# Per-head softmax over selected keys: maxima found two heads ahead, four tables each for keys and queries, a ring of three bias tiles

## What is computed

```python
def dsa_attention(q, k, v, qi, ki, wi, rel_bias, n_keep):
    def block(args):                       # 128 queries at a time
        ...
        _, idx = lax.top_k(score, n_keep)
        ksel = gather(k, idx); vsel = gather(v, idx)
        rel = qpos[None, :, None] - idx
        bias = jnp.moveaxis(rel_bias[t5_bucket_2(rel)], -1, 2)
        logits = jnp.einsum('bqhd,bqkhd->bqhk', qb, ksel) * (A_HEAD_DIM ** -0.5)
        logits = jnp.where((rel >= 0)[:, :, None, :], logits + bias, -jnp.inf)
        p = jax.nn.softmax(logits, axis=-1).astype(v.dtype)
        return jnp.einsum('bqhk,bqkhd->bqhd', p, vsel)
```

## Time and profile before

| | |
|---|---|
| median of 3 executions | 2489.11 us (2487.56 to 2490.77) |
| the profiled execution, first to last instruction | 2486.1 us |
| the stage's loop in it, first score to last mix | about 1133.8 to 1215.9 us, 82 us |
| busy over the whole span | PE 94%, PEld 87%, DVE 43%, ACT 40%, POOL 26% |
| mean granted TensorE clock | 0.968 |

### The profile page before, as it was taken

How to read it: one execution, slowest core, us unless ns; L and a number is a source line. 1 busy time by engine, 2 the same in 40 slices (tenths; PEclk the granted TensorE clock), 3 DMA queues, 4 the chain that set the end, 5 groups by cost and what they waited for, 6 DMA issues and landing times. The chain is left out here.

```text
span 2486.1 us, 40279 instructions
## 1 busy us (share of the span) xinstructions
PE 2329.6 (94%) x17224; PEld 2161.8 (87%) x17224; DVE 1076.9 (43%) x1571; ACT 987.5 (40%) x1440; POOL 647.8 (26%) x505
## 2 busy tenths in 40 slices
PE   7997898997899999898999999998999999999999
PEld 6995588985589997796799999998888879999998
DVE  2438624537532114596534434433334333543443
ACT  5237543246633325425524313324544433432332
POOL 1002222112222704436304302313221211320331
PEclk9999999998999999998999999999999989999999
DMA  5323022310022220122033233322111002323322
GB/s 179 117 90 93 1 69 81 97 54 5 1 90 69 69 78 18 52 77 78 27 98 89 75 101 93 88 88 85 35 35 38 32 33 70 99 74 109 94 73 81
DMA packets 235233, 175.94 MB, mean 71 GB/s; under 512 B 7732, under 2 KB 230060, under 8 KB 234544
## 3 DMA queue, kind: packets, MB, share of 16 engines
q1 hardware_dynamic: 235056, 173.37, 23.1%
HBM read 171.20 MB, written 10.09 MB: 73 GB/s over the span
## 5 line engine op out<-in xcount | busy, mean ns | idle before, releaser
L326 DVE TENSOR_TENSOR panel_lo<-panel_raw,panel_hi 128x2048 fp32r<-128x2048 f32 (+2 forms) x150 | 327.7, 2185 | 421.1 <-ACT panel_hi L318 421.1
L318 ACT ACTIVATE panel_hi<-panel_raw 128x2048 fp32r<-128x2048 f32 (+2 forms) x155 | 276.1, 1781 | 431.3 <-PE product L407 295.9
L407 PE MATMUL product<-scaled_hi,panel_hi 128*128 128x264 f32 (+2 forms) x1408 | 287.4, 285 | 8.3 <-DVE scaled_lo L3645 5.4
L420 PE MATMUL product_banks<-panel_hi,scaled_hi 128*128 128x256 f32 x1008 | 284.8, 282 | 4.0 <-DVE scaled_lo L3645 3.2
L407 PE MATMUL product<-scaled_lo,panel_hi 128*128 128x264 f32 (+2 forms) x1408 | 285.2, 284 | 0.0
L420 PE MATMUL product_banks<-panel_hi,scaled_lo 128*128 128x256 f32 x1008 | 284.7, 282 | 0.0
L420 PE MATMUL product_banks<-panel_lo,scaled_hi 128*128 128x256 f32 x1008 | 284.4, 282 | 0.0
L407 PE MATMUL product<-scaled_hi,panel_lo 128*128 128x264 f32 (+2 forms) x1408 | 284.2, 283 | 0.0
L407 PEld LDWEIGHTS product<-scaled_hi,panel_hi 128*128 128x128 f32 x1408 | 218.6, 190 | 9.1 <-issue 5.8
L407 PEld LDWEIGHTS product<-scaled_lo,panel_hi 128*128 128x128 f32 x1408 | 219.1, 189 | 0.0
L407 PEld LDWEIGHTS product<-scaled_hi,panel_lo 128*128 128x128 f32 x1408 | 218.8, 190 | 0.0
(11 more groups left out here) (478 smaller groups left out, 5309.7 us busy)
## 6 DMA issues: line engine op xcount, KB each, us to landing
panel_raw<-in_w_in_dram SPq DMA_DIRECT2D x26, 1024.0 KB, 5.3
panel_raw<-in_ffn_w_gate_dram SPq DMA_DIRECT2D x44, 512.0 KB, 4.0
panel_raw<-in_ffn_w_up_dram SPq DMA_DIRECT2D x44, 512.0 KB, 5.3
panel_raw<-in_ffn_w_down_dram SPq DMA_DIRECT2D x32, 704.0 KB, 4.5
panel_raw<-in_even_w_in_dram SPq DMA_DIRECT2D x21, 1024.0 KB, 5.1
panel_raw<-in_odd_w_in_dram SPq DMA_DIRECT2D x12, 1024.0 KB, 5.1
panel_raw<-in_w_out_dram SPq DMA_DIRECT2D x8, 1024.0 KB, 5.1
panel_raw<-in_even_w_out_dram SPq DMA_DIRECT2D x8, 768.0 KB, 4.7
```

The source lines that it names most:

```text
L318: act.activation(c.hi[g % 2][:, 0:used], c.raw[g % 2][:, 0:used], ACT.Copy).then_inc(c.hi_made.sem, 1)
L326: dve.tensor_tensor(c.lo[g % 2][:, 0:used], c.raw[g % 2][:, 0:used], c.hi[g % 2][:, 0:used].bitcast(F32), ALU.subtract).then_inc(c.lo_made ...
L407: done = pe.matmul(to, weight(w, k), a[:, k, u:v], start=(k == 0 and x == 0), stop=(k == chunks - 1 and x == 2))
L420: done = pe.matmul(out[:, 0, 0:v - u], a[:, k, at:at + P], w[:, k, u:v], start=(k == 0 and x == 0), stop=(k == chunks - 1 and x == 2))
```

## The change

Four edits.

1. **The maxima are scored two heads ahead.** In iteration i the PE scores head i+2, where it scored i+1. The loops start at i = -2. DVE's `largest` goes with the scores and `low_query`, `key_high` and `query_high` are called for head i+3. `keys` and `query` become rings of four (two more tables of their own in SBUF; the pads of eight tables are cleared in place of six).
2. **The turning moves.** `turn_max(i+1)` stands first in PE's iteration i, so behind `mix(i-2, 4)` and `mix_first(i-2)` of the iteration before it. It turns what was scored in the iteration before.
3. **The copy of the row moves with it.** `max_row(i+1)` stands first in ACT's iteration i, ahead of `take_first(i-2)` and `logarithm(i-2)`. `score_keys(i, 1)` waits for it as well (the count at `min(i+2, H)`), and `turn_max(h)` waits for `sum_added` at 2(h-1), since both use the spare columns of `z`.
4. **`row_bias` becomes a ring of three.** `add_mask` of tile n waits for `largest` of tile n-3, where it waited for n-2.

So in after i = -2 and -1 hold scores alone, i = 0 scores and `score_keys`, i = 1 to 5 all three, i = 6 and 7 `score_keys` and `mix`, i = 8 `mix` alone. POOL's order of work is as it was.

```diff
@@ -2115,15 +2115,16 @@
+    ROWS = 3
...
         slot = [t[:, PAD * n:PAD * (n + 1)] for t in (*c.hi, *c.lo) for n in range(3)]
-        slot += [c.sb(f"selected_slot{n}", [P, PAD], F32R, into=stage)[:] for n in range(2)]
-        keys, query, keys_low, query_low = slot[0:3], slot[3:6], slot[6:10], slot[10:14]
+        slot += [c.sb(f"selected_slot{n}", [P, PAD], F32R, into=stage)[:] for n in range(4)]
+        keys, query, keys_low, query_low = (slot[4 * n:4 * n + 4] for n in range(4))
...
         e = [c.sb(f"selected_e{j}", [P, Stick.WIDE], into=stage) for j in range(2)]
-        row_bias = [c.sb(f"selected_bias{j}", [P, TOK], into=stage) for j in range(2)]
+        row_bias = [c.sb(f"selected_bias{j}", [P, TOK], into=stage) for j in range(ROWS)]
@@ -2176,12 +2177,13 @@
...
                         v = min(u + 512, x)
-                        done = pe.matmul(scores[:, at + u:at + v], query[h % 3][:, b * P:(b + 1) * P], keys[h % 3][:, u:v], start=True, stop=True)
+                        done = pe.matmul(scores[:, at + u:at + v], query[h % 4][:, b * P:(b + 1) * P], keys[h % 4][:, u:v], start=True, stop=True)
                     done.then_inc(c.head_scored.sem, 1)

                 def turn_max(h):
                     pe.wait_ge(c.max_found.sem, c.max_found.at(NB2 * (h + 1)))
                     pe.wait_ge(c.max_row.sem, c.max_row.at(h))
+                    pe.wait_ge(c.sum_added.sem, c.sum_added.at(2 * (h - 1)))
                     if h == 0:
                         pe.wait_ge(c.turned_out.sem, c.turned_out.at(NB2 + 1))
@@ -2200,11 +2202,12 @@
                     if part == 1:
                         pe.wait_ge(c.first_taken.sem, c.first_taken.at(h - 1))
+                        pe.wait_ge(c.max_row.sem, c.max_row.at(min(h + 2, H)))
                     started = None
                     for bank, t, u, n, place in pieces(part):
...
@@ -2231,31 +2234,30 @@

                 for t in range(NB2):
                     turn_mask(t)
-                for i in range(-1, H + 1):
-                    ahead, behind = i + 1 < H, i >= 1
+                for i in range(-2, H + 1):
+                    ahead, behind = i + 2 < H, i >= 1
+                    if 0 <= i + 1 < H:
+                        turn_max(i + 1)
                     if ahead:
-                        score(i + 1, 0)
-                        score(i + 1, 1)
+                        score(i + 2, 0)
+                        score(i + 2, 1)
                     if 0 <= i < H:
                         score_keys(i, 0)
                     if ahead:
-                        score(i + 1, 2)
+                        score(i + 2, 2)
                     if 0 <= i < H:
                         score_keys(i, 1)
                     if behind:
                         mix(i - 1, 0)
                     if ahead:
-                        score(i + 1, 3)
+                        score(i + 2, 3)
                     if behind:
                         mix(i - 1, 1)
                     if ahead:
-                        score(i + 1, 4)
+                        score(i + 2, 4)
                     if behind:
                         mix(i - 1, 2)
                         mix(i - 1, 3)
-                    if ahead:
-                        turn_max(i + 1)
-                    if behind:
                         mix(i - 1, 4)
                         mix_first(i - 1)
                 stream(c, pe, turn, 3)
...
@@ -2321,22 +2323,22 @@
                 act.activation(eye[:], c.eye, ACT.Copy).then_inc(c.stick_constants.sem, 1)
                 for t in range(NB2):
                     place_mask(t)
-                for i in range(-1, H + 2):
+                for i in range(-2, H + 2):
+                    if 0 <= i + 1 < H:
+                        max_row(i + 1)
                     if i >= 2:
                         take_first(i - 2)
                         logarithm(i - 2)
-                    if i + 2 < H:
-                        key_high(i + 2)
+                    if i + 3 < H:
+                        key_high(i + 3)
                     if i >= 2:
                         invert(i - 2)
                     if 0 <= i < H:
                         exponential(i, 0)
-                    if i + 2 < H:
-                        query_high(i + 2)
+                    if i + 3 < H:
+                        query_high(i + 3)
                     if 0 <= i < H:
                         exponential(i, 1)
-                    if i + 1 < H:
-                        max_row(i + 1)
                 invert_first()
...
@@ -2400,23 +2402,23 @@
...
-                for i in range(-1, H + 2):
-                    if i + 1 < H:
-                        largest(i + 1, 0)
-                        largest(i + 1, 1)
+                for i in range(-2, H + 2):
+                    if i + 2 < H:
+                        largest(i + 2, 0)
+                        largest(i + 2, 1)
...
-                    if i + 2 < H:
-                        low_query(i + 2)
+                    if i + 3 < H:
+                        low_query(i + 3)
...
-                    pool.wait_ge(c.max_found.sem, c.max_found.at(n - 1))
+                    pool.wait_ge(c.max_found.sem, c.max_found.at(n - ROWS + 1))
...
```

More of the change, by code:

```diff
@@ L2206, in score_keys @@
                         k = seen(t) - t * P
-                        pe.matmul(out, keys[h % 3][:, at], query[h % 3][:, u:u + n], start=bank != started, stop=False, skip_group_check=True)
+                        pe.matmul(out, keys[h % 4][:, at], query[h % 4][:, u:u + n], start=bank != started, stop=False, skip_group_check=True)
                         started = bank
@@ L2265, in key_high @@
                 def key_high(h):
-                    act.wait_ge(c.keys_scored.sem, c.keys_scored.at(2 * (h - 2)))
+                    act.wait_ge(c.keys_scored.sem, c.keys_scored.at(2 * (h - 3)))
                     for rows in (rows_of(h), others_of(h)):
-                        act.activation(keys[h % 3][rows, 0:TOK], source(h, 1), ACT.Copy).then_inc(c.keys_hi.sem, 1)
+                        act.activation(keys[h % 4][rows, 0:TOK], source(h, 1), ACT.Copy).then_inc(c.keys_hi.sem, 1)
                 def query_high(h, to=None):
-                    for to in (query[h % 3], query_low[h % 4]) if to is None else [to]:
+                    for to in (query[h % 4], query_low[h % 4]) if to is None else [to]:
                         if h == 0 and to is query_low[0]:
@@ L2353, in low_query @@
                     dve.wait_ge(c.head_hi.sem, c.head_hi.at(2 * h + 1))
-                    dve.tensor_tensor(query[h % 3][others_of(h), 0:TOK], source(h, 0), query[h % 3][rows_of(h), 0:TOK].bitcast(F32),
+                    dve.tensor_tensor(query[h % 4][others_of(h), 0:TOK], source(h, 0), query[h % 4][rows_of(h), 0:TOK].bitcast(F32),
                                       ALU.subtract).then_inc(c.head_lo.sem, 1)
@@ L2365, in largest @@
                     hold(dve, c.dve_passed)
-                    dve.tensor_tensor_reduce(row_bias[n % 2][:, 0:x], scores[:, at:at + x], row_bias[n % 2][:, 0:x],
+                    dve.tensor_tensor_reduce(row_bias[n % ROWS][:, 0:x], scores[:, at:at + x], row_bias[n % ROWS][:, 0:x],
                                              -1.0, 3.0e38, ALU.add, ALU.min, found[:, b, col:col + 1]).then_inc(c.max_found.sem, 1)
@@ L2402, in _ @@
                 dve.wait_ge(c.rows_cleared.sem, c.rows_cleared.at(1))
-                for i in range(-1, H + 2):
-                    if i + 1 < H:
-                        largest(i + 1, 0)
-                        largest(i + 1, 1)
+                for i in range(-2, H + 2):
+                    if i + 2 < H:
+                        largest(i + 2, 0)
+                        largest(i + 2, 1)
                     if 0 <= i < H:
                         add_bias(i, 0)
-                    if i + 1 < H:
-                        largest(i + 1, 2)
+                    if i + 2 < H:
+                        largest(i + 2, 2)
                     if 0 <= i < H:
                         add_bias(i, 1)
-                    if i + 1 < H:
-                        largest(i + 1, 3)
-                        largest(i + 1, 4)
+                    if i + 2 < H:
+                        largest(i + 2, 3)
+                        largest(i + 2, 4)
                     if i >= 2:
                         finish(i - 2)
-                    if i + 2 < H:
-                        low_query(i + 2)
+                    if i + 3 < H:
+                        low_query(i + 3)
                 for n in range(2):
@@ L2436, in low_keys @@
                     rows = rows_of(h)
-                    pool.tensor_tensor(keys_low[h % 4][rows, 0:TOK], source(h, 1), keys[h % 3][rows, 0:TOK].bitcast(F32),
+                    pool.tensor_tensor(keys_low[h % 4][rows, 0:TOK], source(h, 1), keys[h % 4][rows, 0:TOK].bitcast(F32),
                                        ALU.subtract).then_inc(c.keys_lo.sem, 1)
@@ L2450, in add_mask @@
```

(2 more changed lines are left out.)

## The result

The changed kernel is slower by about 0.2%: the ratio of its times to those of the kernel before is 1.0021, with a 95% interval from 1.0012 to 1.0029 (medians 2497.28 and 2492.43 us over 20 executions each; the kernel before ran again beside it). That is 5.2 us, from 3.0 to 7.2. One execution of after, 2872.43 us at a granted clock of 0.74, is a slow one and stands outside of the ratio. Forecast were 6.4 us, counted from a median of 2489.11 over three executions; with twenty the same kernel has 2492.43, so it is the difference and not the 2495.5 that can be compared.

The account below looks back on a forecast made before the run. Prediction: a PE-then-DVE loop ending in `low_query` sets the pace. Opening -1.0, clock's iterations -0.1 and +1.6, steady part -0.2 and +0.8, end +5.25: +6.35, from 2489.1 to 2495.5 us; range 2491.5 to 2499.0.

Parts of the forecast that it names:

- What bounds the kernel: Steady loop of 8.57 us: PE 3.3, then DVE 5.2 ending in `low_query`; turning and copy not in it.
- Steady part moved: worth zero: Turning and copy moved, steady iterations: no gain, since the next score still waits for `low_query`.
- Ring of three: Third `row_bias` tile: opening 1.0 us earlier, but POOL's larger tile delays `low_query` in steady iterations, +0.8 in all.
- The collision: `low_query` on DVE held by POOL's 384-column tile: 0.28 us later in each of three iterations, +0.8.
- i = 0 and i = 1: First iterations two heads ahead: -0.1 us for i = 0, +1.6 for i = 1, slowed by half clock.
- The end: From head 7's last `largest` to the last mix: 16.5 us where before took 11.28, +5.25.
- M(1)-M(2): Between the starts of the last `largest` of heads 1 and 2 (i = 0): 10.3 us, -0.1.
- M(0)-M(1): Between the starts of the last `largest` of heads 0 and 1: stays 10.6 us, set by POOL.
- (1): Rival: the clock stays up through i = 1; -2.3 us, to 2493.2; chance 0.13.
- (2; e3): Rival: the turning was in the way, steady loop falls to PE's own work; -3.2 us, to 2492.3; chance 0.12.
- (3): Rival, slower still: copy holds `score_keys(i, 1)` each iteration, or low clock reaches into i = 2; 2498.5 us; chance 0.10.
- (4): Rival, faster than before: shifted gaps meet the clock differently further on in the program; about 2483 us; chance 0.05.

Follow-up runs that it names:

- e1: The changed kernel with the `row_bias` ring back at two tiles; stage 92.64 us, against 91.20 for the changed kernel.
- e9: The kernel before with a ring of three, `low_query` ahead of the last `largest`, and useless matmuls around head 1's last scores; stage 85.17 us, against 85.98.
- e4: The changed kernel with `low_query` moved ahead of the last `largest` on DVE; stage 90.13 us, against 91.20 for the changed kernel.
- e2: The kernel before with only the `row_bias` ring raised to three tiles; stage 86.40 us, against 85.98 for the kernel before.
- e3: The changed kernel with the turning and the copy of the row back at their old places; stage 91.02 us, against 91.20 for the changed kernel.
- e7: The changed kernel with four useless matmuls around head 2's last scores in i = 0; stage 88.54 us, against 91.20 for the changed kernel.
- e8: The kernel before with four useless matmuls around head 1's last scores in i = 0; ratio 0.9978 to before, stage 84.16 us against 85.98.
- e10: e9 plus POOL's mask of head 1's last block made earlier and small useless matmuls in i = -1; ratio 0.9985 to the kernel before, stage 83.31 us.

## Why the prediction was right, point by point

- **What bounds the kernel.** "Neither the turning nor the copy is in it": right in what it decided, since both edits gained nothing in the steady part. It was read too simply. `low_query` was last, but the copy was only 0.05 from holding `score_keys`, which the prediction did not compare. e1 and e9 show each bound alone, at 8.55 and 8.56 in the mean, and only with both out of the way (e4) does the pace fall to 8.08, of which 0.30 is PE's wait for the fourth `largest`.
- **Steady part moved: worth zero.** Right for i = 3 to 5 (e1, without the third tile, has 8.55). For i = 2, which has no `low_query` behind a `finish` before it, I took off 0.17 and it was 0.51 (8.07 from 8.55): there the copy had been the only bound (in before it ends at 1164.01 and `score_keys` starts at 1164.27, with `low_query` done at 1163.17), and two ahead removes it. This term was mis-sized by 0.3.
- **Ring of three.** Opening -1.0, measured -1.09. The collision +0.28 an iteration, measured 0.20 (8.78 against 8.57), `low_query` 0.95 to 1.09. Right in place and nearly in size. e1 and e2 show it both ways.
- **i = 0 and i = 1.** -0.1 and +1.6, measured -0.46 and +1.48. In e1, e3 and e4 the same two intervals run from 9.67 to 10.54. That the half clock is the cause of the long i = 1 is shown by e7. The size of both terms depends on when the clock rises, and the prediction had no means to tell that: that +1.6 met +1.48 is in part luck. In e1, with the same mechanism, it would have been +2.0, and in e3 +1.3.
- **The end.** 16.5, measured 16.55. The hold of 0.26 for the copy was 0.1.
- **The sum** was 6.35, measured 5.22: 0.4 from M(1)-M(2), 0.1 each from M(0)-M(1), the opening and M(2)-M(3), 0.3 from M(3)-M(4), 0.2 from the collision. All are small and, but for 0.02 at the end, to the same side, so none hides another.
- **The rivals.** The clock did not stay up by itself (1). The turning was not in the way (2; e3), though the copy was one step behind. The wait of `score_keys(i, 1)` for the copy never showed (3). Nothing made the program faster (4); the mean clock was 0.964 against 0.968.

## What to carry to other kernels

Running a producer one iteration further ahead is paid with an iteration more: what ran side by side once runs in turn, at the front and at the end. With eight heads that was 5 to 6 us, so each of five iterations would have had to give back more than 1 us, where PE's idle in one was 0.8 in all and the best order (e4) gave back 0.5. And before a step is moved off the critical path, the second-longest path is to be measured too: here two bounds lay within a few hundredths of each other, so removing either alone gained nothing (`low_query` in e9, the copy in e1), and letting POOL run one tile further (e2) made the first one worse.

## What the runs showed of the hardware

- Four matmuls without use in PE's gaps kept the clock at 2.4 GHz, where without them it fell to 1.2 for 6 to 7 us: 1.8 to 2.2 us for one gap of 1.6 and one of 1.0 (e7, e8). In the kernel before the program was 0.22% faster with them (0.10 to 0.34%), of which the stage explains 0.07%. The change costs 0.21%, so the two are of one size.
- A DVE instruction with two SBUF operands (`low_query`, 64 x 528, 0.70 alone) took up to 1.10 behind a POOL tile of 384 columns (e3) and 1.44 behind POOL's `low_keys` (e10). It holds POOL as well when it starts first: POOL's tile of 256 columns, 0.73 alone, took 1.18 at 1162.59 of before, where `low_query` had started at 1162.47. The other DVE instructions of the stage, with one operand in PSUM, stayed within some hundredths in all traces (`largest` of 528 columns 0.71 each time).
- The same 1130 us of program ahead of the stage ended anywhere from 1127.9 to 1137.3 us in the fourteen traces. A single time of this kernel says nothing on 5 us; the stage's own time, from its own start, does.
